# Moving attention's square sum, weight pieces and adds in a one-core hybrid encoder layer

## The chip, the cores and the metric

The kernel runs on one core of one Trainium2 chip. The metric is device time in microseconds (us) of one execution; the figure given is the median of several runs.

## The reference

One layer over 1024 rows of width 1024: a combined input projection, a spatial gating unit and a sliding-window attention side by side, each normalised and sent through one output projection, then a SwiGLU feed-forward part and a final norm.

```python
h = rms_norm(x, mix_norm_g[l])
proj = h @ w_in[l]
u_a, v_a, q, k, v = jnp.split(proj, splits, axis=-1)
y_a = spatial_gating(u_a, v_a, sgu_ln_g[l], sgu_ln_b[l], sgu_w[l], sgu_b[l])
y_b = window_sink_attention(q, k, v, sinks[l], rel_bias)
y_a = rms_norm(y_a, group_norm_g[l, :D_A])
y_b = rms_norm(y_b, group_norm_g[l, D_A:])
x = x + jnp.concatenate([y_a, y_b], axis=-1) @ w_out[l]
h = rms_norm(x, ffn_norm_g[l])
x = x + (jax.nn.silu(h @ w_gate[l]) * (h @ w_up[l])) @ w_down[l]
...
return rms_norm(x, final_norm_g)
```

## The kernel before, in words

Every fp32 product is made of three matmuls on parts rounded to fp32r: high by high, high by low, low by high (`split_mm`, L853 to L855). ScalarE makes a high part by a copy, VectorE the low part by a subtraction. So each operand is a raw tile, a ScalarE operation and a VectorE operation, and TensorE waits on a counting semaphore for the last of them.

The work of each of the five engines (TensorE, VectorE, ScalarE, POOL, and SyncE, which issues nearly all DMAs) is written out by hand, one list each, and each engine goes through its list in order. Nothing is scheduled by a program. The wide matrix products (input projection of u and q, feed-forward, down projection) use a Strassen scheme with seven products P1 to P7, taken in the order P1, P2, P6, P5, P7, P3, P4. In the input part each product has four pieces i (0 and 1 are columns of q, 2 and 3 of u). P4 takes them in the order 2, 3, 0, 1.

Stages in time: gated values v and keys (to 75 us), input products with the spatial mixing (to 163 us), attention rows r = 0 to 7 interleaved with the output projection (to 285 us), the feed-forward products, the down projection.

The names that matter here, by engine.

- **TensorE.** After P4's last piece come the transposes of row 0's probabilities (`probs_T`, L1033), the logits of row 1 (L1021), the values of row 0 (L1044), and `ya_totals(0)`, which transposes the sum of squares of the gated rows. Then the output projection: `out_unit(r, n)` is 12 matmuls, n = 0, 1 on the gated half with `woA`, n = 2, 3 on the attention half with `woB`. After three of these come `probs_T(1, 0)`, `logits(2)`, `probs_T(1, 1)` and `yb_rows(0)` (L1051), which transposes POOL's sum of attention squares, and then `ya_totals(1)`.
- **VectorE.** `d_to_lo` (L1843) makes low parts of the Strassen row sums D, `product_add` (L1859) adds products in PSUM onto earlier ones, `corner` (L1875, L1877) scales a finished block, `in_weight_lo` (L1837) makes low parts of weights, `add_bias`, `maxima` and `normal_probs` (L1973, L1984, L1998) are attention's softmax, `woA_piece` and `woB_piece` (L1780, L2010) the low parts of the four pieces of each half of the output weight. Each `woA_piece` and `woB_piece` raises `wo_split` by one. `ya_lo_rows` (L1883) makes the gated rows' low part.
- **ScalarE.** `probabilities` (exponentials, L1451), `probs_to_sbuf` (L1463), `yb_to_sbuf` (L1469), `ya_square`, `ya_hi_rows`, and the high part `woB_piece` (L1496), which waits until both halves of its `woB_raw` tile have landed.
- **POOL.** `gate(g)` (L707) multiplies the gated unit, `ya_sum(n)` (L714) sums its squares, `yb_sums(r)` (L770, L774) sums the squares of attention row r in two steps, `rootA`, `root` make the inverse roots.
- **SyncE.** Its list around here: load `woA` pieces 2 and 3, then `xr[0]` and `xr[1]`, rows of x for the residual, which lie on the same memory as the raw `woA` tiles and wait for them, then `xr[2]`, then the eight half loads of `woB_raw`:

```python
for i in range(2):
    sp.wait_ge(wo_split, 3 + i)
    sp.dma_start(xr[i][:], xt[i]).then_inc(x_in[i], 16)
sp.wait_ge(prod_done, in_at("P3", 3))
sp.dma_start(xr[2][:], xt[2]).then_inc(x_in[2], 16)
for t in IN_ORDER["P4"]:
    sp.wait_ge(prod_done, in_at("P4", t))
    for g in range(KV):
        ...
        sp.dma_start(woB_raw[t][g * DH:(g + 1) * DH, :], w_out[row:row + DH, :]).then_inc(block_in[t], 16)
```

Of the kernel before, what the change touches and what calls it, by code (L numbers as in the profile page):

```python
# [24 lines left out]
def hybrid_trunk_layer(nc, x, xT, mix_gT, w_in, sgu_ln_g, sgu_ln_b, sgu_w, sgu_b, sinks, rel_bias,  # L25
# [201 lines left out]
    YA_TOTAL_AT = ((2, 4), (1, 6))  # L227
# [73 lines left out]
    with ExitStack() as ctx:  # L301
        ps = ctx.enter_context(nc.psum_tensor("ps", [P, 8, C], F32))

        def sem(name):
# [11 lines left out]
        x_sq, x_mse, x_rstd, rstd_T, roots_ready, hT_hi_ready, hT_ready = (  # L316
            sem(n) for n in ("x_sq", "x_mse", "x_rstd", "rstd_T", "roots_ready", "hT_hi_ready", "hT_ready"))
# [45 lines left out]
        def _(sp):  # L363
# [5 lines left out]
            def xT_load(h, k):  # L369
                if h:  # L370
                    sp.wait_ge(hT_hi_ready, k + 1)
                sp.dma_start(hT_raw[h][:, k, :], xT[h, k]).then_inc(block_in[k], 16)
# [266 lines left out]
        def _(pool):  # L639
# [69 lines left out]
            def ya_sum(n):  # L709
# [4 lines left out]
                combine(V[:, dst], V[:, dst], V[:, src], ALU.add).then_inc(ya_summed, 1)  # L714
# [25 lines left out]
            ya_sum(4)  # L740
            ya_sum(5)
# [35 lines left out]
            rootA(1)  # L777
            for r in range(T):
# [9 lines left out]
                if r + 2 < T:  # L788
                    yb_sums(r + 1)
            for n, m in SUMS[0][2:5]:  # L790
# [58 lines left out]
        def _(pe):  # L849
# [29 lines left out]
            for k in range(2):  # L879
                pe.wait_ge(hT_hi_ready, k + 1)  # L880
# [91 lines left out]
            def ya_totals(half):  # L972
                slot, summed = YA_TOTAL_AT[half]
# [5 lines left out]
                for t in range(HT):  # L979
                    last = nc.tensor.transpose(ps[:, 7, t * P:(t + 1) * P], V[:, slot, t * P:(t + 1) * P], ident[:])  # L980
# [145 lines left out]
            ya_totals(1)  # L1126
            for r in range(T):
# [7 lines left out]
                if r + 1 < T:  # L1135
# [5 lines left out]
                    values(r + 1)  # L1141
                    if 0 < r < T - 2:
# [90 lines left out]
        def _(act_e):  # L1233
# [6 lines left out]
            def xT_block(h, k):  # L1240
                act_e.wait_ge(block_in[k], LOADED[k] + 16 * h)
                if h == 0 and k == 0:
                    act_e.wait_ge(wv0_in, 32)
# [22 lines left out]
            for k in range(K):  # L1266
                wv_block(k)
                xT_block(0, k)
# [171 lines left out]
            ya_square(3)  # L1440
            ya_hi_rows(3)
            in_weight_hi("P4", 2)
# [110 lines left out]
            ya_hi_rows(4)  # L1553
            ya_square(5)
            ya_hi_rows(5)
            u_gelu(7)
            probs_to_sbuf(0, 0)
# [189 lines left out]
        def _(dve):  # L1747
# [3 lines left out]
            def xT_lo(h, k):  # L1751
                dve.wait_ge(hT_hi_ready, K * h + k + 1)
# [49 lines left out]

            for k in range(K):
# [149 lines left out]
            for k in range(1, 4):  # L1953
                d_to_lo("D4", k)
            woA_piece(2)
            product_add("P3", 0)
            corner("P3", 0)
            in_weight_lo("P4", 0)
# [3 lines left out]
            woA_piece(3)  # L1962
            product_add("P3", 2)

# [43 lines left out]
            def woB_piece(t):  # L2008
                dve.wait_ge(wo_hi_ready, HA + t + 1)
                stt(woB_lo[:, t, :], woB_raw[t][:], grp_g[:, HA + t:HA + t + 1], woB_hi[:, t, :].bitcast(F32), ALU.mult, ALU.subtract).then_inc(wo_split, 1)  # L2010
# [301 lines left out]
```

## Time and profile before

| | |
|---|---|
| median of 3 runs | 927.34 us (927.29 to 927.34) |
| the profiled execution's own time | 927.43 us |
| its span in the trace | 925.6 us |
| TensorE busy | 913.2 us, 99% |
| VectorE busy | 588.2 us, 64% |
| ScalarE busy | 430.5 us, 47% |
| POOL busy | 402.2 us, 43% |
| TensorE's mean granted clock | 0.998 of full speed |

Busy time is time in which an engine executes; matmuls overlap each other in the trace, so that a matmul of 0.39 us follows the one before after 0.23 us. The span runs from the first to the last instruction in the trace; the execution's own time has some 1.8 us more around it.

### The profile page before, as it was taken

The numbers are of one execution on the slowest core, as the hardware profiler recorded it, in microseconds if no ns is written. First come the engines' busy times: TensorE is split into PE (matmuls) and PEld (weight loads), VectorE is DVE, ScalarE is ACT, GpSimd is POOL, SyncE is SP. The second block draws the span as 40 slices with busy tenths as digits, with TensorE's granted clock in tenths as the row PEclk, the third lists the DMA queues.
The fourth block names the chain that finished last, engine by engine and source line by source line (L and its number), as shares of the span: only waits on it lengthen the run. The fifth ranks groups of instructions, "written<-read, shape, count | busy, mean of one in ns | idle before, by whom it ended". The sixth has DMA issues, their size and how long they took to land.

```text
span 925.6 us, 11960 instructions
## 1 busy us (share of the span) xinstructions
PE 913.2 (99%) x4229; PEld 748.9 (81%) x4229; DVE 588.2 (64%) x776; ACT 430.5 (47%) x837; POOL 402.2 (43%) x392
## 2 busy tenths in 40 slices
PE   9999999899999999999999999999999999999997
PEld 7888887677878878888888888888888888888885
DVE  5659878877677876364464745646446666544753
ACT  6647547775655633332333333333334354444351
POOL 2459633622224388566585564955754000000022
PEclk9999999999999999999999999999999999999999
DMA  9787454112233352725527355273457996656543
GB/s 332 252 242 229 115 162 145 35 57 80 89 108 101 114 170 92 243 88 194 174 98 240 99 174 183 91 239 121 152 190 265 350 385 197 199 189 199 187 139 133
DMA packets 151487, 158.56 MB, mean 171 GB/s; under 512 B 27576, under 2 KB 109060, under 8 KB 151428
## 3 DMA queue, kind: packets, MB, share of 16 engines
q1 hardware_dynamic: 150756, 157.40, 52.5%
q8 instruction: 34, 0.56, 0.2%
q10 hardware_dynamic: 672, 0.40, 0.1%
q14 instruction: 25, 0.20, 0.1%
HBM read 117.26 MB, written 40.50 MB: 170 GB/s over the span
## 4 chain that ended last, share of the span: by engine, by line
PE 87%; DVE 4%; issue 3%; ACT 3%; POOL 2%; DMA 1%; DVEq 0%; POOLq 0%; ACTq 0%
PE ps L853 27%; PE ps L855 27%; PE ps L854 27%; ACT S L1451 1%; PE ps L969 1%; PE ps L1044 1%; PE ps L1116 1%; PE ps L1021 1%; PE ps L1033 1%; DVE P_lo L2086 1%; DMA A22s<-in_w_gate 1%; DVE woA_lo L1780 0%; POOL V L714 0%; PE ps L877 0%; DVE T_lo L2073 0%
## 5 line engine op out<-in xcount | busy, mean ns | idle before, releaser
L2086 DVE TENSOR_TENSOR P_lo<-P_raw,P_hi 128x512 fp32r<-128x512 f32 x132 | 120.8, 931 | 83.5 <-ACT P_hi L1545 76.2
L853 PE MATMUL ps<-T_hi,P_hi 128*128 128x512 f32 x352 | 137.1, 390 | 0.0
L855 PE MATMUL ps<-T_hi,P_lo 128*128 128x512 f32 x352 | 137.0, 389 | 0.0
L854 PE MATMUL ps<-T_lo,P_hi 128*128 128x512 f32 x352 | 136.9, 389 | 0.0
L797 POOL TENSOR_TENSOR wd<-wd 128x256 f32<-128x256 f32 x88 | 81.2, 923 | 93.8 <-DMA wd<-in_w_down 88.6
L853 PE MATMUL ps<-rb_hi,ra_hi 128*128 128x512 f32 x308 | 119.8, 389 | 0.0
L854 PE MATMUL ps<-rb_lo,ra_hi 128*128 128x512 f32 x308 | 119.8, 389 | 0.0
L855 PE MATMUL ps<-rb_hi,ra_lo 128*128 128x512 f32 x308 | 119.8, 389 | 0.0
L1659 ACT ACTIVATE ra_hi<-ra 128x512 fp32r<-128x512 f32 x77 | 48.6, 632 | 98.4 <-DMA rb<-w_down_T 59.6
L647 POOL TENSOR_SCALAR late<-late 128x1 f32<-128x1 f32 x12 | 5.5, 458 | 193.4 <-ACT junk L1727 177.2
L2182 DVE TENSOR_TENSOR ra_lo<-ra,ra_hi 128x512 fp32r<-128x512 f32 x77 | 55.2, 718 | 37.2 <-ACT ra_hi L1659 37.0
L1545 ACT ACTIVATE P_hi<-P_raw 128x512 fp32r<-128x512 f32 x132 | 76.6, 620 | 3.5 <-POOL P_raw L756 3.5
L853 PEld LDWEIGHTS ps<-T_hi,P_hi 128*128 128x128 f32 x352 | 66.1, 188 | 14.3 <-issue 0.7
L855 PEld LDWEIGHTS ps<-T_hi,P_lo 128*128 128x128 f32 x352 | 66.1, 188 | 13.9
L854 PEld LDWEIGHTS ps<-T_lo,P_hi 128*128 128x128 f32 x352 | 66.1, 188 | 13.6
L1650 ACT ACTIVATE G<-G 128x512 f32<-128x512 f32 x33 | 20.9, 632 | 112.4 <-DVE G L2162 112.4
L853 PE MATMUL ps<-B,P_hi 128*128 128x512 f32 x176 | 69.0, 392 | 0.1
L855 PE MATMUL ps<-B,P_lo 128*128 128x512 f32 x176 | 68.5, 389 | 0.0
L854 PE MATMUL ps<-B,P_hi 128*128 128x512 f32 x176 | 68.5, 389 | 0.0
L854 PEld LDWEIGHTS ps<-rb_lo,ra_hi 128*128 128x128 f32 x308 | 57.8, 188 | 12.1
L853 PEld LDWEIGHTS ps<-rb_hi,ra_hi 128*128 128x128 f32 x308 | 57.8, 188 | 12.1
L855 PEld LDWEIGHTS ps<-rb_hi,ra_lo 128*128 128x128 f32 x308 | 57.8, 188 | 11.8
(272 smaller groups left out, 2028.0 us busy)
## 6 DMA issues: line engine op xcount, KB each, us to landing
wd<-in_w_down SPq DMA_DIRECT2D x44, 256.0 KB, 3.4
w_down_T<-wd SPq DMA_DIRECT2D x22, 512.0 KB, 4.8
ra<-act_S SPq DMA_DIRECT2D x44, 256.0 KB, 2.7
rb<-w_down_T SPq DMA_DIRECT2D x44, 256.0 KB, 3.0
act_S<-Q SPq DMA_DIRECT2D x33, 256.0 KB, 3.7
ra<-act_A SPq DMA_DIRECT2D x33, 256.0 KB, 4.9
rb<-in_w_down SPq DMA_DIRECT2D x33, 256.0 KB, 5.7
P_raw<-in_w_gate SPq DMA_DIRECT2D x22, 256.0 KB, 3.6
```

Of the source, the lines that this page charges most:

```text
L797: nc.gpsimd.tensor_tensor(wd[:, d, :], wd[:, x, :], wd[:, y, :], ALU.subtract).then_inc(wd_summed, 1)
L853: mm(dst, lhs[0], rhs[0], start=start, stop=False, skip_group_check=onto)
L854: mm(dst, lhs[0], rhs[1], start=False, stop=False, skip_group_check=onto)
L855: return mm(dst, lhs[1], rhs[0], start=False, stop=stop, skip_group_check=onto)
L969: last = mm(ps[:, MIX_BANK[m % 2], t * P:(t + 1) * P], vn[:, h, HT * half + t], sgu_wT[:, h, :], start=True, stop=True)
L1021: last = mm(ps[:, 3 + g, (2 * ci + tp) * P:(2 * ci + tp + 1) * P], q, kT[rows, c * CH:c * CH + WIN], start=True, stop=True)
L1033: last = nc.tensor.transpose(ps[:, 5, (2 * g + tp) * P:(2 * g + tp + 1) * P], S[:, g, ci, tp, :], ident[:])
L1545: actv(w_h[p, m][:], src[:], ACT.Copy).then_inc(w_hi_ready, 1)
L1650: actv(g[:], g[:], ACT.Silu).then_inc(silu_done, 1)
L1659: actv(ra_hi[n][:], ra[n][:], ACT.Copy).then_inc(step_hi, 1)
L2086: tt(w_l[p, m][:], src[:], w_h[p, m][:].bitcast(F32), ALU.subtract).then_inc(w_split, 1)
L2182: tt(ra_lo[n][:], ra[n][:], ra_hi[n][:].bitcast(F32), ALU.subtract)
```

## The change

It has seven parts.

1. At the start VectorE, not ScalarE, makes the first block of `hT_hi`, with a semaphore of its own (`hT0_hi_ready`); the counts of `hT_hi_ready` fall by one where they are waited for.
2. VectorE: `product_add("P3", 0)` and its corner move ahead of D4's pieces 2 and 3, `in_weight_lo("P4", 2)` ahead of `add_bias(0)`.
3. VectorE: `woA_piece(2)` and `woA_piece(3)` move from among P3's adds to behind `normal_probs(0)`.
4. ScalarE: `in_weight_hi("P4", 2)` moves ahead of `ya_hi_rows(3)`, `probs_to_sbuf(0, 0)` ahead of `ya_square(5)`.
5. POOL: `yb_sums(0)` moves ahead of `ya_sum(4)` and `ya_sum(5)`, the latter writes to `roots[1]` now, and `rootA(1)` moves into the loop of rows.
6. TensorE: `ya_totals(1)` moves behind `values(1)`, and VectorE's `ya_total_sums(1)` behind `yb_lo(1)`.
7. VectorE's `woB_piece(2)` waits for all gated sums, since its low part lies on their memory.

VectorE before, from the second D4 piece of P3's time to the end of `maxima(0)`; `woA_lo` is `woA_piece`, `U` P3's sum, `s_lo` P4's weight parts, `S` the logits:

```order
L1843 TENSOR_TENSOR D_lo<-D_raw,D_hi 128x512 [waits combo_hi] x3
L1780 SCALAR_TENSOR_TENSOR woA_lo<-raw_75,small,woA_hi 128x1024 [waits wo_hi_ready]
L1859 TENSOR_TENSOR U<-ps,U 128x512 [waits c_summed,copied,prod_done]
...
L1780 SCALAR_TENSOR_TENSOR woA_lo<-raw_76,small,woA_hi 128x1024 [waits wo_hi_ready]
L1859 TENSOR_TENSOR U<-ps,U 128x512 [waits c_summed,copied,prod_done]
L1973 TENSOR_TENSOR S<-ps,bias 128x512 [waits logits_done,sinks_ready,bias_in]
L1973 TENSOR_TENSOR S<-ps,bias 128x512
L1979 MEMSET S 128x2x64 [waits s_added]
L1979 MEMSET S 128x2x64
L1837 TENSOR_TENSOR s_lo_150<-s_2_114,wB_hi_138 128x512 [waits w_hi_ready,s_added]
```

VectorE with the change, from the end of the normalisation of row 0 (L2011) to the bias of row 1 (L1986):

```order
L2008 RECIPROCAL small<-small 128x8 [waits den_ready]
L2011 TENSOR_TENSOR S<-S,small 128x1024 [waits rden_ready]
L1790 SCALAR_TENSOR_TENSOR woA_lo<-raw_75,small,woA_hi 128x1024 [waits wo_hi_ready]
L1790 SCALAR_TENSOR_TENSOR woA_lo<-raw_76,small,woA_hi 128x1024 [waits wo_hi_ready]
L1896 TENSOR_TENSOR ya<-vn,ya 128x4x128 [waits ya_hi_ready]
L1888 SCALAR_TENSOR_TENSOR qT_153<-ps,roots_81 128x8x64 [waits prod_done]
L1896 TENSOR_TENSOR ya<-vn,ya 128x4x128 [waits ya_hi_ready]
L1888 SCALAR_TENSOR_TENSOR qT_153<-ps,roots_81 128x8x64 [waits prod_done]
L1986 TENSOR_TENSOR S<-ps,bias 128x512 [waits logits_done,p_T]
```

Both `woA` pieces have left the first place and stand in the second, behind the normalisation.

SyncE's queue, the same before and with the change (172 to 174 are `xr[0]` to `xr[2]`, 168 to 171 `woB_raw[0]` to `[3]`):

```order
L464 DMA xr_172<-in_x 128x1024 [waits wo_split]
L464 DMA xr_173<-in_x 128x1024 [waits wo_split]
L466 DMA xr_174<-in_x 128x1024 [waits prod_done]
L471 DMA woB_raw_170<-in_w_out 64x1024 [waits prod_done]
L471 DMA woB_raw_170<-in_w_out 64x1024
L471 DMA woB_raw_171<-in_w_out 64x1024 [waits prod_done]
L471 DMA woB_raw_171<-in_w_out 64x1024
L471 DMA woB_raw_168<-in_w_out 64x1024 [waits prod_done]
L471 DMA woB_raw_168<-in_w_out 64x1024
```

Nothing moved in it; the first two rows wait for the two `woA` pieces.

POOL before, from the inverse root of the first half to the sum of the first attention row:

```order
L649 TENSOR_TENSOR small<-small 128x4 [waits msA_ready]
L714 TENSOR_TENSOR V<-V 128x512 [waits ya_summed,ya_squared] x2
L770 TENSOR_TENSOR yb_sq<-yb_sq 128x256 [waits yb_squared]
L774 TENSOR_TENSOR yb_sum_162<-yb_sq 128x128 [waits yb_halved]
L647 TENSOR_SCALAR small<-small 128x4 [waits ssqA_ready]
```

and with the change:

```order
L649 TENSOR_TENSOR small<-small 128x4 [waits msA_ready]
L771 TENSOR_TENSOR yb_sq<-yb_sq 128x256 [waits yb_squared]
L775 TENSOR_TENSOR yb_sum_162<-yb_sq 128x128 [waits yb_halved]
L716 TENSOR_TENSOR V<-V 128x512 [waits ya_summed,ya_squared]
L716 TENSOR_TENSOR roots_81<-V 128x512 [waits c_out,ya_summed,ya_squared]
L647 TENSOR_SCALAR small<-small 128x1 [waits yb_totalled]
```

The two gated sums now come behind the attention squares.

The diff (the declaration of the new semaphore left out):

```diff
--- before.py
+++ after.py
@@ -224,7 +224,7 @@
     SQUARE_TO = (1, 0, 2, 3, 0, 3, 0, 3)
     YA_SUMS = ((1, 0, 2), (2, 3, 4), (2, 0, 5), (2, 3, 6), (1, 0, 7), (1, 3, 8))
     YA_ROWS = (2, 3, 4, 5, 0, 1, 6, 7)
-    YA_TOTAL_AT = ((2, 4), (1, 6))
+    YA_TOTALS = ((V[:, 2], 4), (roots[1], 6))
 
     IN_PRODUCTS, W_SPLITS, W_SUMS, D_SPLIT, IN_COPIES, IN_ADDS = 32, 30, 16, 16, 12, 16
 
@@ -368,7 +368,7 @@
 
             def xT_load(h, k):
                 if h:
-                    sp.wait_ge(hT_hi_ready, k + 1)
+                    sp.wait_ge(hT_hi_ready, max(k, 1))
                 sp.dma_start(hT_raw[h][:, k, :], xT[h, k]).then_inc(block_in[k], 16)
 
             def item_load(n):
@@ -711,7 +711,9 @@
                 pool.wait_ge(ya_squared, squared)
                 if n:
                     pool.wait_ge(ya_summed, n)
-                combine(V[:, dst], V[:, dst], V[:, src], ALU.add).then_inc(ya_summed, 1)
+                if n == 5:
+                    pool.wait_ge(c_out, corner_at("P4", 1))
+                combine(roots[1][:] if n == 5 else V[:, dst], V[:, dst], V[:, src], ALU.add).then_inc(ya_summed, 1)
 
             def rootA(half):
                 cs = slice(HT * half, HT * half + HT)
@@ -737,8 +739,7 @@
             gate(6)
             gate(7)
             rootA(0)
-            ya_sum(4)
-            ya_sum(5)
+
             def w_sum(i, n, m):
                 sub = nc.gpsimd.tensor_tensor
                 if n == "S1":
@@ -774,7 +775,8 @@
                 nc.gpsimd.tensor_tensor(yb_sum4[:], yb_sq[:, 0], yb_sq[:, 1], ALU.add).then_inc(yb_summed, 1)
 
             yb_sums(0)
-            rootA(1)
+            ya_sum(4)
+            ya_sum(5)
             for r in range(T):
                 if r == T - 1:
                     pool.wait_ge(out_done, out_at(T - 1, 1))
@@ -787,6 +789,8 @@
                 root(ssqB[:, r:r + 1], msB[:, r:r + 1], rB[:, r:r + 1], DA, msB_ready, rB_ready, r + 1)
                 if r + 2 < T:
                     yb_sums(r + 1)
+                if r == 0:
+                    rootA(1)
             for n, m in SUMS[0][2:5]:
                 w_sum(0, n, m)
 
@@ -877,7 +881,10 @@
                 nc.tensor.transpose(ps[:, 0, 0:P], ident[:], ident[:])
 
             for k in range(2):
-                pe.wait_ge(hT_hi_ready, k + 1)
+                if k:
+                    pe.wait_ge(hT_hi_ready, k)
+                else:
+                    pe.wait_ge(hT0_hi_ready, 1)
                 pe.wait_ge(wv_hi_ready, k + 1)
                 for t in range(HT):
                     mm(ps[:, t, :], hT_hi[0][:, k, t * P:(t + 1) * P], wv_hi[:, k], start=k == 0, stop=False)
@@ -970,14 +977,14 @@
                 last.then_inc(mix_done, 1)
 
             def ya_totals(half):
-                slot, summed = YA_TOTAL_AT[half]
+                total, summed = YA_TOTALS[half]
                 pe.wait_ge(ya_summed, summed)
                 if half == 0:
                     pe.wait_ge(c_out, corner_at("P4", 3))
                 else:
                     pe.wait_ge(ssqA_ready, 1)
                 for t in range(HT):
-                    last = nc.tensor.transpose(ps[:, 7, t * P:(t + 1) * P], V[:, slot, t * P:(t + 1) * P], ident[:])
+                    last = nc.tensor.transpose(ps[:, 7, t * P:(t + 1) * P], total[:, t * P:(t + 1) * P], ident[:])
                 last.then_inc(ya_total, 1)
 
             def value_windows(w):
@@ -1123,7 +1130,6 @@
             logits(2)
             probs_T(1, 1)
             yb_rows(0)
-            ya_totals(1)
             for r in range(T):
                 if 0 < r < T - 1:
                     probs_T(r + 1, 0)
@@ -1139,6 +1145,8 @@
                     if r == T - 2:
                         h2_transposed(r - 1, 0)
                     values(r + 1)
+                    if r == 0:
+                        ya_totals(1)
                     if 0 < r < T - 2:
                         h2_transposed(r - 1, 1)
                 out_unit(r, 2)
@@ -1239,8 +1247,6 @@
 
             def xT_block(h, k):
                 act_e.wait_ge(block_in[k], LOADED[k] + 16 * h)
-                if h == 0 and k == 0:
-                    act_e.wait_ge(wv0_in, 32)
                 actv(hT_hi[h][:, k, :], hT_raw[h][:, k, :], ACT.Copy, scale=mix_g[:, k:k + 1]).then_inc(hT_hi_ready, 1)
 
             def wv_block(k):
@@ -1265,7 +1271,8 @@
             act_e.dma_start(mix_g, mix_gT).then_inc(wv0_in, 16)
             for k in range(K):
                 wv_block(k)
-                xT_block(0, k)
+                if k:
+                    xT_block(0, k)
             for r in range(HT):
                 xT_block(1, 2 * r)
                 square(r)
@@ -1438,8 +1445,8 @@
             ya_square(2)
             ya_hi_rows(2)
             ya_square(3)
+            in_weight_hi("P4", 2)
             ya_hi_rows(3)
-            in_weight_hi("P4", 2)
             in_weight_hi("P4", 3)
 
             def probabilities(r):
@@ -1551,10 +1558,10 @@
             u_gelu(6)
             ya_square(4)
             ya_hi_rows(4)
+            probs_to_sbuf(0, 0)
             ya_square(5)
             ya_hi_rows(5)
             u_gelu(7)
-            probs_to_sbuf(0, 0)
             probs_to_sbuf(0, 1)
             woB_piece(0)
             yb_to_sbuf(0)
@@ -1749,7 +1756,10 @@
             copy = nc.vector.tensor_copy
 
             def xT_lo(h, k):
-                dve.wait_ge(hT_hi_ready, K * h + k + 1)
+                if h or k:
+                    dve.wait_ge(hT_hi_ready, K * h + k)
+                else:
+                    dve.wait_ge(hT0_hi_ready, 1)
                 stt(hT_lo[h][:, k, :], hT_raw[h][:, k, :], mix_g[:, k:k + 1], hT_hi[h][:, k, :].bitcast(F32), ALU.mult, ALU.subtract).then_inc(hT_ready, 1)
 
             def wv_block(k):
@@ -1800,6 +1810,9 @@
                                   sinks_rep[rows].rearrange("p (g a b) -> p g a b", g=KV, a=2)[:, :, :, t2], -1.0, None, ALU.mult)
                 last.then_inc(sinks_ready, 1)
 
+            dve.wait_ge(wv0_in, 32)
+            dve.wait_ge(block_in[0], LOADED[0])
+            ts(hT_hi[0][:, 0, :], hT_raw[0][:, 0, :], mix_g[:, 0:1], None, ALU.mult).then_inc(hT0_hi_ready, 1)
             for k in range(K):
                 wv_block(k)
                 xT_lo(0, k)
@@ -1950,17 +1963,17 @@
             woA_piece(1)
             product_add("P7", 3)
             corner("P7", 3)
-            for k in range(1, 4):
-                d_to_lo("D4", k)
-            woA_piece(2)
+            d_to_lo("D4", 1)
             product_add("P3", 0)
             corner("P3", 0)
+            d_to_lo("D4", 2)
+            d_to_lo("D4", 3)
             in_weight_lo("P4", 0)
             product_add("P3", 1)
             corner("P3", 1)
             in_weight_lo("P4", 1)
-            woA_piece(3)
             product_add("P3", 2)
+            in_weight_lo("P4", 2)
 
             def add_bias(r):
                 if r == 0:
@@ -2007,6 +2020,8 @@
 
             def woB_piece(t):
                 dve.wait_ge(wo_hi_ready, HA + t + 1)
+                if t == 2:
+                    dve.wait_ge(ya_summed, 6)
                 stt(woB_lo[:, t, :], woB_raw[t][:], grp_g[:, HA + t:HA + t + 1], woB_hi[:, t, :].bitcast(F32), ALU.mult, ALU.subtract).then_inc(wo_split, 1)
 
             def add_out(r, n):
@@ -2086,7 +2101,6 @@
                 tt(w_l[p, m][:], src[:], w_h[p, m][:].bitcast(F32), ALU.subtract).then_inc(w_split, 1)
 
             add_bias(0)
-            in_weight_lo("P4", 2)
             maxima(0)
             in_weight_lo("P4", 3)
             corner("P3", 2)
@@ -2097,6 +2111,8 @@
             ya_lo_rows(3)
             corner("P4", 3)
             normal_probs(0)
+            woA_piece(2)
+            woA_piece(3)
             ya_lo_rows(4)
             corner("P4", 0)
             ya_lo_rows(5)
@@ -2118,8 +2134,6 @@
                     add_out(r + 1, 0)
                 if r + 1 < T:
                     yb_totals(r)
-                if r == 0:
-                    ya_total_sums(1)
                 if r + 2 < T:
                     add_bias(r + 2)
                     maxima(r + 2)
@@ -2131,6 +2145,8 @@
                         h2_lo(r - 1, 0)
                     add_out(r + 1, 1)
                     yb_lo(r + 1)
+                if r == 0:
+                    ya_total_sums(1)
                 add_out(r, 2)
                 if r + 2 < T:
                     normal_probs(r + 2)
```

## Rows read from the trace of the kernel before

**Rows 1.** The page's first part: busy us, share of the span, instructions.
```profile
PE 913.2 (99%) x4229; PEld 748.9 (81%) x4229; DVE 588.2 (64%) x776; ACT 430.5 (47%) x837; POOL 402.2 (43%) x392
```
**Rows 2.** Waits of TensorE: waiter, releaser, us in total, times, longest.
```profile
PE ps L1051 <- POOL yb_sum L774: 2.0, 1, 2.0
...
PE ps L1033 <- ACT pT L1463: 1.1, 1, 1.1
PE ps L853 <- DVE U L1859: 0.5, 1, 0.5
PE ps L853 <- DVE s_lo L1837: 0.3, 1, 0.3
```
**Rows 3.** Timeline of the start (start us, us, what); VectorE's TENSOR_SCALAR; xT's first landing.
```profile
4.23 0.71 ACT L1244 ACTIVATE hT_hi<-hT_raw,small 128x512 fp32r<-128x512 f32 x1
...
4.99 0.80 PE L883 MATMUL ps<-wv_hi,hT_hi 128*128 128x512 f32 x1
L1769 DVE TENSOR_SCALAR vn<-v_sb,small x8: 516/548/1559, 34.1 to 56.8; 128x512 f32<-128x512 f32 x8
DMA to landing us min/median/max: 3.0/3.0/3.0
```
**Rows 4.** Timeline of SyncE's queue, DMA issues at the start and 143 to 165 us.
```profile
1.17 0.42 SPq L372 DMA_DIRECT2D hT_raw<-in_xT  x1
...
143.24 5.38 SPq L464 DMA_DIRECT2D xr<-in_x  x2
...
154.29 9.75 SPq L471 DMA_DIRECT2D woB_raw<-in_w_out  x8
```
**Rows 5.** The loads of woB_raw: ns min/median/max of one issue, and landing.
```profile
L471 SPq DMA_DIRECT2D woB_raw<-in_w_out x8: 466/552/597, 154.3 to 163.4; - x8
DMA to landing us min/median/max: 3.4/3.8/4.2
```
**Rows 6.** Windows: full queue; one xr load; one pair of woB_raw. Last: DMA share, GB/s.
```profile
18.00:20.00 2.00, 2.00 (x11) 1.65 (x10) 0.75 (x1) 1.44 (x4) 1.25 (x5) 1.00 1.06 407
144.00:147.00 3.00, 3.00 (x14) 2.25 (x16) 2.96 (x6) 3.00 (x6) 0.00 (x0) 1.00 0.55 175
155.00:158.00 3.00, 3.00 (x15) 2.48 (x14) 2.97 (x7) 2.97 (x10) 0.00 (x0) 1.00 0.70 175
```
**Rows 7.** Timeline of VectorE, 146 to 164 us, in order of time.
```profile
146.99 1.28 DVE L1780 SCALAR_TENSOR_TENSOR woA_lo<-raw,small,woA_hi 128x1024 fp32r<-128x1024 f32 x1
...
156.38 0.69 DVE L1883 TENSOR_TENSOR ya<-vn,ya 128x512 fp32r<-128x512 f32 x1
158.06 1.23 DVE L1998 TENSOR_TENSOR S<-S,small 128x1024 f32<-128x1024 f32 x1
161.65 1.84 DVE L1883 TENSOR_TENSOR ya<-vn,ya 128x512 fp32r<-128x512 f32 x1 [2.37 <-ACT ya L1356]
```
**Rows 8.** Timeline of POOL, 147 to 178 us.
```profile
147.33 2.09 POOL L714 TENSOR_TENSOR V<-V 128x512 f32<-128x512 f32 x1 [5.87 <-ACT V L1364]
158.34 3.35 POOL L707 TENSOR_TENSOR vn<-vn,U 128x512 f32<-128x512 f32 x2 [8.91 <-ACT U L1343]
161.65 2.98 POOL L714 TENSOR_TENSOR V<-V 128x512 f32<-128x512 f32 x2
...
173.79 3.60 POOL L714 TENSOR_TENSOR V<-V 128x512 f32<-128x512 f32 x2 [2.63 <-ACT V L1364]
```
**Rows 9.** Timeline of ScalarE, 165 to 177 us.
```profile
165.18 1.14 ACT L1496 ACTIVATE woB_hi<-woB_raw,small 128x1024 fp32r<-128x1024 f32 x1
166.80 0.60 ACT L1469 ACTIVATE yb_raw<-ps 128x512 f32<-128x512 f32 x1 [0.48 <-PE ps L1044]
...
176.22 0.57 ACT L1463 ACTIVATE pT<-ps 128x512 f32<-128x512 f32 x1
```
**Rows 10.** Timeline of TensorE, 175 to 180 us.
```profile
175.39 0.60 PE L1033 MATMUL ps<-ident,S 128*128 128x128 f32 x4
...
179.65 0.33 PE L1051 MATMUL ps<-ident,yb_sum 128*128 128x128 f32 x1 [1.98 <-POOL yb_sum L774]
```

More of the change, by code:

```diff
@@ L315, in hybrid_trunk_layer @@
         x_in = [sem(f"x_in{s}") for s in range(4)]
-        x_sq, x_mse, x_rstd, rstd_T, roots_ready, hT_hi_ready, hT_ready = (
-            sem(n) for n in ("x_sq", "x_mse", "x_rstd", "rstd_T", "roots_ready", "hT_hi_ready", "hT_ready"))
+        x_sq, x_mse, x_rstd, rstd_T, roots_ready, hT0_hi_ready, hT_hi_ready, hT_ready = (
+            sem(n) for n in ("x_sq", "x_mse", "x_rstd", "rstd_T", "roots_ready", "hT0_hi_ready", "hT_hi_ready", "hT_ready"))
         block_in = [sem(f"block_in{k}") for k in range(K)]
```

## The prediction

> **What bounds the kernel now.** I read the page's first part, the waits of TensorE, and then the timelines of the stretch that they point to. TensorE is busy 913.2 of 925.6 us [rows 1], so an edit can only give back time in which TensorE stands, or add some. It stands little: 2.0 us for POOL's sum of the attention squares (L774), 1.1 us for ScalarE's copy of the probabilities (L1463), 0.5 and 0.3 us for two VectorE operations [rows 2]. All four lie between 143 and 180 us, where attention, the last input products and the first output products overlap. After 200 us no TensorE wait is listed at all, so whatever is lost or won before 180 us stays to the end. The change aims at these four and at the start.
>
> **The start.** Today ScalarE makes both operands of the first matmul in turn, the second, `hT_hi`, at 4.23 us for 0.71, and TensorE begins at 4.99 [rows 3]. Now VectorE makes `hT_hi[0]` with one TENSOR_SCALAR, whose usual length is 548 ns. It can't start before its block lands, and the earliest xT block takes 3.0 us from its issue at 1.17 [rows 3, 4], so 4.2 us. It ends at 4.75 and TensorE starts at about 4.8: **-0.2 us**. The bounds are 0 (the block lands late; VectorE then also does the two low parts later) and -0.5 (a landing at 3.7).
>
> **The four waits, if nothing else moved.** VectorE adds P3's row 0 before two of the D4 pieces and `woA_piece(2)` (-0.5). P4's third low part is made before attention's bias (-0.3), ScalarE copies the probabilities before the fifth square (-1.1), and POOL does the attention squares' sum before the two gated sums that take 3.60 us from 173.79 [rows 8] (-2.0). That is 3.9 us at most. The totals of the second half are transposed later with the same four matmuls: nothing gained or lost. The new wait of VectorE's `woB_piece(2)` for the sixth gated sum costs nothing: the gated sums come straight behind the attention squares and end 3.6 us later, and VectorE has the bias and the maxima of row 2 to do first. POOL's new wait on `c_out` is for a corner that stands ahead of row 1's bias in VectorE's list, and is long done.
>
> **What is behind the moved weight pieces.** `woA_piece(2)` and `(3)` go from the middle of P3 to behind the first row's normalisation. They are 1.28 us each [rows 7], but they also raise `wo_split` to 3 and 4, and SyncE's queue waits for exactly these before it loads `xr[0]` and `xr[1]`, since these lie on the raw weights. SyncE works in order. Today it issues the two `xr` loads from 143.24 on, the second at the end of 5.38 us, and then the eight `woB_raw` loads from 154.29 to 164.04, each as P4's products finish [rows 4]. Now all eight stand behind the fourth `woA` piece. ScalarE's next operation after the probabilities' copy is `woB_piece(0)`, on the sixth of them; today it runs at 165.18 without a wait [rows 9].
>
> When is the fourth piece done? The normalisation (L1998) starts at 158.06 and ends at 159.29 [rows 7]. Ahead of it VectorE loses a 1.28 us piece, but P4's third low part must now wait for ScalarE and for POOL's sum at 147.33 to 149.42 [rows 8], so I put its end only 0.3 earlier, at 159.0. Without interference the pieces are done at 159.0 + 2 x 1.2 = 161.4. But POOL is in its gates then (158.34, x2 in 3.35) and in sums from 161.65 [rows 8], and VectorE operations that read two SBUF tensors don't run beside POOL's: `ya_lo`, started at 161.65 together with POOL's sum, took 1.84 us, where the same operation at 156.38, with POOL idle, took 0.69 [rows 7, 8]. With one POOL operation of 1.15 us slipped in ahead of each piece it is **163.7**. I take this, since POOL has six operations queued there. The Trainium skill (GPSIMD Engine Reference, "8. Key points") says that GpSimd shares its SBUF interfaces with VectorE and contends with VectorE instructions of two SBUF inputs. By that rule both pieces are caught, the later of the two times.
>
> When does `woB_raw[0]` land? Behind the fourth piece stand `xr[1]`, `xr[2]` (0.33 us an issue) and three pairs of `woB` loads (0.55 each) [rows 4, 5]; the second half of piece 0 is issued 0.7 + 5 x 0.55 = 3.45 us later and lands 3.8 after that [rows 5]: 163.7 + 7.2 = 170.9 by issue alone. By bytes: `xr[1]`'s data begin 1.5 us after its issue, at 165.2, and five half-megabytes go before piece 0 is complete. By DMA time used they cost 3.0 x 0.55 = 1.65 us for an `xr` and 3.0 x 0.70 = 2.1 for a `woB` pair [rows 6], 9.6 in all: 174.8. At the 407 GB/s of a full queue [rows 6] 2.62 MB take 6.4: 171.6. Between 171.6 and 174.8 I take **172.8**. With the undisturbed 161.4 the same three are 168.6, 169.3 and 172.5. The Trainium skill (DMA: Bandwidth & Descriptors, "Anatomy of one DMA") gives about 2 us and bytes at 436 GB/s; for one `xr` load that is 3.2 us, as the row has it. By its rate the five take 6.0 us, the landing is 171.2 and the sum below would be 930.4, an estimate from that page.
>
> From there the order of ScalarE is fixed. `woB_piece(0)` at 165.18 to the copy of row 1's probabilities at 176.22 is 11.04 us, less 0.48 that it waited for TensorE, plus the copy's 0.57 [rows 9]; TensorE's transposes follow 0.15 later and the yb transposes 0.4 behind them. So TensorE gets to L1051 at landing + 11.7 = 184.5, where it now gets there at 179.65 [rows 10]: +4.85. It stops on the way first at row 1's probabilities (now 175.39, without a wait), since these hang on the same ScalarE work. What was won in the four waits is swallowed: TensorE is early and then stands longer. POOL's squares' sum is then hidden in it.
>
> **Sum:** 927.43 (the profiled execution) + 4.85 - 0.2 = 932.1; the median of the three runs is 0.1 lower, so **932.0**.
>
> **Rivals.**
> *Faster, the four waits go (8%).* If piece 0 lands before 167.9 (landing + 11.7 before 179.65), the loads decide nothing or little. With a landing at 165 or sooner the price is 927.3 - 3.9 - 0.2 = 923.2. For it speaks that VectorE has an idle 2.37 us before 161.65 [rows 7] into which both pieces fit, and that the queue is otherwise empty. Against it: even with these pieces undisturbed the issue times alone give 168.6. Only if VectorE came through its stretch more than 0.7 us sooner than I put it could this happen.
> *No change (14%).* VectorE keeps the port, the fourth piece ends at 161.4, and the loads are bound by issue, or go at 407 GB/s: landing 168.6 to 169.3, +0.65 to +1.35, less 0.2: 927.8 to 928.5.
> *Slower, but by VectorE and POOL themselves.* POOL's gates 4 and 5 could get in ahead of the normalisation, since ScalarE's GELU comes earlier too: then all of the above moves 1.2 us on, to 933.2, and with the slow DMA price to 935.2. This is inside my forecast (78% in all); it is its upper end.
>
> **Range and chances.** 0.2% is 1.85 us, about what a measurement tells from no change. The forecast covers 928.9 to 935.2 (landings of 170 to 176); half of the "no change" case is taken in by going down to 928.4. Slower by over 0.2% 0.78, within it 0.14, faster 0.08.
>
> **What the profile after would show.** SyncE's `xr[1]` issue at about 163.7, some 15 us later than now, and the `woB_raw` loads bunched from 164 to 168; ScalarE standing 6 to 10 us before L1503 (the `woB_hi` piece) for a DMA; TensorE standing some 5 to 7 us before the transposes of row 1's probabilities, and the yb_sum wait gone; nothing changed after 200 us but the shift. I am wrong if ScalarE's `woB_piece(0)` still starts before 168, and the size is wrong if the landing is off my 172.8, about one for one.

## Result and the profile after

The changed kernel takes 936.1 us (median of 5 runs, 935.66 to 936.47), the kernel before 927.34 (927.29 to 928.36): ratio 1.009 [1.008, 1.010] (the brackets are a 95% interval), 8.8 us slower. The forecast was 932.0, between 928.4 and 935.2: the direction held, the size was short by 4.1, and the measured time lies 0.9 above the upper end. The profiled execution of the changed kernel took 935.74 us, 8.31 more than the one of before; all that follows is made against that 8.31.

The page's first part, and the granted clock in 40 slices, of the changed kernel:

```profile
PE 914.3 (98%) x4229; PEld 750.5 (80%) x4229; DVE 588.5 (63%) x777; ACT 430.1 (46%) x836; POOL 402.3 (43%) x392
...
PEclk9999999899999999999999999999999999999999
```

The busy times are those of [rows 1] within 1.6 us; the span has grown, so the shares of TensorE, VectorE and ScalarE are each a point lower. The eighth slice of the clock, 163 to 187 us at 23.3 us a slice, has fallen to 8. Waits of TensorE after (waiter, releaser, us in total, times, longest):

```profile
PE ps L1040 <- DVE S L2011: 9.7, 2, 8.6
PE ps L881 <- POOL ident L643: 1.5, 1, 1.5
PE ps L857 <- DVE ya L1896: 1.4, 1, 1.4
```

The four waits of [rows 2] are gone; one of 8.6 us, for row 1's normalisation (L2011), has come, and two small ones: 1.1 us for row 0's normalisation and 1.4 for the gated rows' low part. (The 1.5 us for `ident` is at the very start and is in every run.) What lies behind the long one is read backwards. ScalarE (start us, us, what, idle before):

```profile
162.48 0.60 ACT L1470 ACTIVATE pT<-ps 128x512 f32<-128x512 f32 x1 [1.03 <-PE ps L1040]
174.75 1.15 ACT L1503 ACTIVATE woB_hi<-woB_raw,small 128x1024 fp32r<-128x1024 f32 x1 [11.66 <-DMA woB_raw<-in_w_out]
```

It stands 11.66 us for a load, where it had none to wait for at 165.18 [rows 9]. SyncE's queue, and the loads' time from issue to landing:

```profile
160.80 2.56 SPq L464 DMA_DIRECT2D xr<-in_x  x2
163.40 0.43 SPq L466 DMA_DIRECT2D xr<-in_x  x1
163.88 4.98 SPq L471 DMA_DIRECT2D woB_raw<-in_w_out  x8
DMA to landing us min/median/max: 5.3/7.0/8.6
```

The eight half loads, issued over 9.75 us as P4's products ended [rows 4], now go within 4.98, and land after 5.3 to 8.6 us instead of 3.4 to 4.2 [rows 5]. VectorE and POOL at the two weight pieces:

```profile
156.29 2.25 DVE L2011 TENSOR_TENSOR S<-S,small 128x1024 f32<-128x1024 f32 x1
158.47 4.54 DVE L1790 SCALAR_TENSOR_TENSOR woA_lo<-raw,small,woA_hi 128x1024 fp32r<-128x1024 f32 x2
```

```profile
156.17 3.52 POOL L707 TENSOR_TENSOR vn<-vn,U 128x512 f32<-128x512 f32 x2 [8.96 <-ACT U L1350]
159.66 4.48 POOL L716 TENSOR_TENSOR V<-V 128x512 f32<-128x512 f32 x2
```

The pieces take 4.54 us and POOL's sums 4.48 beside them, which both had in less (1.28 a piece [rows 7], 2.98 for the two sums [rows 8]). TensorE in the end:

```profile
183.46 1.11 PE L1040 MATMUL ps<-ident,S 128*128 128x128 f32 x4 [8.55 <-DVE S L2011]
184.51 2.08 PE L1028 MATMUL ps<-kT,qT 64*128 64x128 f32 x16
...
187.43 0.42 PE L1058 MATMUL ps<-ident,yb_sum 128*128 128x128 f32 x1
```

It gets to the yb transposes at 187.43 where it got there at 179.65 [rows 10]: +7.78. The same four transposes of `S` take 1.11 us, not 0.60 [rows 10], and the windows (from and to in us, length, busy us and instructions of TensorE, its weight loads, VectorE, ScalarE and POOL) say why (last three columns: granted clock, DMA share, GB/s):

```profile
174.00:179.00 5.00, 0.91 (x5) 0.41 (x3) 1.93 (x3) 4.19 (x7) 0.00 (x0) 1.00 0.34 77
179.00:183.00 4.00, 0.00 (x0) 0.00 (x0) 1.81 (x4) 4.00 (x18) 0.77 (x1) 0.55 0.00 0
183.00:189.00 6.00, 5.54 (x29) 4.69 (x30) 4.97 (x7) 4.39 (x6) 5.43 (x6) 0.50 0.01 3
189.00:192.00 3.00, 3.00 (x16) 2.16 (x16) 2.90 (x5) 1.14 (x6) 0.10 (x1) 0.90 0.00 0
```

While TensorE stood, its granted clock fell to the lower level, 0.50 of 2.4 GHz, and stayed there for the first 6 us from 183.

### The profile page after: what moved, and what is told of

Read it like the earlier page. It is cut to its first block, busy times and chain, and to the rows that moved or that the text cites. A ratio compares the mean times of both kernels' runs of the same rounds, so it can differ in the third digit from the quotient of the medians.

```text
span 933.9 us, 11960 instructions
## 1 busy us (share of the span) xinstructions
PE 914.3 (98%) x4229; PEld 750.5 (80%) x4229; DVE 588.5 (63%) x777; ACT 430.1 (46%) x836; POOL 402.3 (43%) x392
## 4 chain that ended last, share of the span: by engine, by line
PE 90%; DVE 4%; issue 2%; ACT 1%; DMA 1%; POOL 1%; SPq 0%; DVEq 0%; POOLq 0%; ACTq 0%
PE ps L857 28%; PE ps L859 28%; PE ps L858 28%; PE ps L1123 1%; DMA woB_raw<-in_w_out 1%; PE ps L1040 1%; PE ps L976 1%; PE ps L1051 1%; PE ps L1028 1%; DVE S L2011 1%; DMA A22s<-in_w_gate 1%; DVE woA_lo L1790 0%; DVE P_lo L2101 0%; PE ps L881 0%; DVE T_lo L2088 0%
```

## Experiments

The kernel before had medians of 927.73, 927.61, 927.59 and 927.10 us in the sessions of these runs; each ratio is to the runs of its own session. The changed kernel's 936.1 was measured beside a 927.34, so the differences to it that follow cross sessions whose medians of the same kernel lie up to 0.4 us apart.

**1. The weight pieces.** Before with only those moved, then the changed kernel with only those put back.

```diff
# e1, on the kernel before
-            woA_piece(2)
             product_add("P3", 0)
...
-            woA_piece(3)
...
             normal_probs(0)
+            woA_piece(2)
+            woA_piece(3)
# e2, on the changed kernel
             normal_probs(0)
-            woA_piece(2)
-            woA_piece(3)
...
             d_to_lo("D4", 3)
+            woA_piece(2)
...
             in_weight_lo("P4", 1)
+            woA_piece(3)
```

> The kernel before with only the two woA pieces of VectorE moved behind the first normalisation. Theory (the queue of SyncE): the loads of woB_raw are held until the fourth piece is done, piece 0 lands near 174 us, ScalarE stands some 9 us before its woB piece and TensorE some 7 to 8 us before the transposes of row 1's probabilities; about 935 to 936 us, as slow as the whole change or slower by little. Rival (VectorE and POOL hold each other up, or the moved POOL sums do it): at most 929 us, with woB_raw landing in time.

> The whole change with the two woA pieces put back among P3's adds. Theory: the loads go out as before, the wait for row 1's probabilities disappears, and what is left are the gains of the other parts: start -1.4, P3's sum and P4's weight -0.8, the probabilities' copy -1.1, POOL's sum -2.0: about 922 us. Rival (another part costs too): above 925 us.

The move alone: 935.51 us, ratio 1.0077 [1.0061, 1.0094]. The pieces put back: 923.82 us, ratio 0.9955 [0.9940, 0.9970]. So the two pieces cost 7.8 us by themselves and 12.3 in the company of the rest, and the rest is worth 3.9 (927.73 to 923.82), which TensorE's long stand swallows. In e1 TensorE waits

```profile
PE ps L1033 <- DVE S L1996: 6.2, 1, 6.2
PE ps L1033 <- ACT pT L1463: 2.1, 1, 2.1
```

and ScalarE's first `woB_hi` starts at 173.48, 11.75 us behind the end of the fourth piece (157.18 + 4.55); in the changed kernel the distance is 11.74.

**2. SyncE's queue.** The changed kernel with the loads of `xr[0]` and `xr[1]` behind the weights' in SyncE's list, so that nothing but P4 holds those up, while the pieces stay where the change put them.

```diff
-            for i in range(2):
-                sp.wait_ge(wo_split, 3 + i)
-                sp.dma_start(xr[i][:], xt[i]).then_inc(x_in[i], 16)
             sp.wait_ge(prod_done, in_at("P3", 3))
...
+            for i in range(2):
+                sp.wait_ge(wo_split, 3 + i)
+                sp.dma_start(xr[i][:], xt[i]).then_inc(x_in[i], 16)
```

> The whole change, with the two xr loads of SyncE put behind the eight woB_raw loads, so that those don't wait for the woA pieces. Theory: woB_raw lands as before, ScalarE doesn't stand, and the time is 924 to 925 us, since TensorE still waits 1.2 us for the normalisation and 1.4 us for ya_lo, which the moved pieces push behind POOL's operations. Rival (the place of the pieces on VectorE is the cost): still above 930 us.

926.86 us, ratio 0.9990 [0.9981, 0.9999]: of the 12.3 us the queue's order gives back 9.2. I had expected 2 to 3 us more. The load's wait is gone (ScalarE starts `woB_hi` at 164.01 without one), but waits for VectorE have stayed:

```profile
PE ps L1040 <- DVE S L2011: 2.8, 2, 1.6
PE ps L857 <- DVE ya L1896: 1.4, 1, 1.4
```

The pieces still hold VectorE for 4.54 us (at 159.50), so that row 1's bias starts at 167.93, where in e2 it starts at 164.52, and its normalisation comes late. Of the 2.8 us, 1.2 are for row 0's normalisation and are in e2 as well; the other 1.6 and the 1.4 for `ya` are the pieces' own price. They match the 3.0 us between e3 and e2. It stood nowhere in my working; in the changed kernel the long stand swallows them.

**3. The clock.** The changed kernel with 76 more transposes of the identity into a bank that is rewritten next, ahead of row 1's transposes, so that TensorE doesn't stand. They add work and change nothing that is computed.

```diff
             out_unit(1, 0)
+            for n in range(76):
+                nc.tensor.transpose(ps[:, 5, 0:P], ident[:], ident[:])
             probs_T(1, 0)
```

> The whole change, with 76 transposes of the identity into a free bank ahead of the transposes of row 1's probabilities, so that TensorE works through most of its 8.6 us wait. Theory: the matmuls after the wait keep their full pace, and some 2 us come back: about 934 us. Rival (the slower pace behind the wait costs nothing that counts): 936 us.

934.12 us, ratio 1.0068 [1.0053, 1.0083], 2.0 less than the changed kernel, though row 1's transposes start no sooner (183.61, against 183.46). From there to the second values it takes 5.87 us, against 7.93. The windows that fell to 0.50 above:

```profile
179.00:183.00 4.00, 4.00 (x39) 4.00 (x37) 1.80 (x4) 4.00 (x18) 0.62 (x1) 1.00 0.00 0
183.00:189.00 6.00, 5.19 (x41) 4.19 (x40) 5.97 (x8) 4.43 (x6) 5.62 (x6) 1.00 0.00 0
```

So the lower clock behind the stand cost 2.0 us on top of the stand itself.

**4. The rate of the weights' loads.** In the changed kernel the `woB_raw` half loads run at 221 to 258 GB/s (168 to 175 us) with all 16 DMA engines busy, where the row of x before them ran at 406. Two edits ask whether the shape is the cause: one transfer of 128 partitions for each weight tile, and two of 64 for each of the first two rows of x.

```diff
# e9, on the changed kernel
-                for g in range(KV):
-                    row = DA + (g * G + t) * DH
-                    sp.dma_start(woB_raw[t][g * DH:(g + 1) * DH, :], w_out[row:row + DH, :]).then_inc(block_in[t], 16)
+                sp.dma_start(woB_raw[t][:], woB_src[:, t]).then_inc(block_in[t], 16)
# ScalarE's count for a tile falls from 32 to 16, and
# woB_src = w_out[DA:DA + KV * G * DH, :].rearrange("(g t d) n -> g t d n", g=KV, t=G)
# e11, on the changed kernel
-                sp.dma_start(xr[i][:], xt[i]).then_inc(x_in[i], 16)
+                for q in range(2):
+                    hp = slice(64 * q, 64 * q + 64)
+                    sp.dma_start(xr[i][hp, :], xt[i][hp, :]).then_inc(x_in[i], 16)
# VectorE's counts for these rows rise by 16
```

> The changed kernel with each tile of the raw weights of the attention half loaded by one transfer of 128 partitions in place of two of 64. Theory (the half transfers drain at 240 GB/s although all 16 DMA engines are busy, since each has only 64 partitions of 4 KB): whole transfers drain nearer the 406 GB/s of the x loads, a tile takes about 1.5 us in place of 2.15, the tile that ScalarE waits for is the third and lands 1.3 to 2 us sooner, and the time is 934.1 to 934.8. Rival (the rate has to do with where the data lie in memory, not with the shape): 936.1 as the changed kernel, and the same 240 GB/s.

> The changed kernel with the first two rows of x for the residual loaded by two transfers of 64 partitions each in place of one of 128; the weights' loads as in the changed kernel. Theory (the shape of 64 partitions sets the 240 GB/s of the weights' half loads, not their source): the second x row, issued at 163, now drains at some 240 GB/s where 406 were seen at 165 to 166, so the weights behind it land about 0.9 us later and the time is about 937. Rival (the rate belongs to the source tensor): the x rows still drain at 400, the landing stays within 0.3 us and the time is 936.1 to 936.4.

The first went wrong in a way that no theory had: 961.86 us, ratio 1.0370 [1.0356, 1.0385]. ScalarE waits until 197.97, and the windows show why:

```profile
170.00:180.00 10.00, 4.89 (x22) 3.73 (x20) 0.35 (x1) 0.00 (x0) 1.22 (x2) 0.94 0.13 52
180.00:190.00 10.00, 0.00 (x0) 0.00 (x0) 0.00 (x0) 0.00 (x0) 0.00 (x0) 0.50 0.13 53
```

A DMA share of 0.13 is two engines of 16. The source of the new transfer has two blocks of 64 rows, so its outermost count is 2. The Trainium skill (DMA: Bandwidth & Descriptors, "Why a DMA increments its semaphore by 16 and not by 1") says that a transfer runs on the largest number of engines, up to 16, that divides the outermost counts of both sides; here that is 2, and the trace agrees. As a test of the rate the run is void.

The second answers it. Bandwidth of the changed kernel at 165 us, one row of x in whole transfers, and of e11 at 165 to 167, the same row in halves:

```profile
165.00:166.00 1.00, 0.14 (x2) 0.00 (x0) 1.00 (x2) 0.00 (x0) 1.00 (x2) 1.00 1.00 406
```

```profile
165.00:166.00 1.00, 0.80 (x6) 0.42 (x4) 1.00 (x3) 0.00 (x0) 1.00 (x1) 1.00 0.86 242
166.00:167.00 1.00, 0.00 (x0) 0.00 (x0) 1.00 (x2) 0.00 (x0) 1.00 (x2) 1.00 1.14 254
```

937.54 us, ratio 1.0112 [1.0096, 1.0127]: 1.4 more than the changed kernel, where 0.9 was expected. The weights land 13.2 us behind the fourth piece in place of 11.7. A half is also a smaller transfer, 256 KB. That isn't the cause: from 5 to 10 us the changed kernel loads tiles of 128x512, 256 KB each over 128 partitions, at 356 GB/s:

```profile
5.00:10.00 5.00, 5.00 (x22) 4.08 (x23) 3.67 (x6) 3.00 (x5) 0.00 (x0) 1.00 1.00 356
```

So the 64-partition shape sets the rate, whatever the source. The Trainium skill (SBUF — State Buffer, "Door 1: The DMA port swizzle") says that partitions 0 to 63, and likewise 64 to 127, reach only 8 of the 16 ports of the memory, some 218 GB/s. The rows show 221 to 258, with halves of both kinds in the queue: somewhat above that figure, and far below 406.

**5. What each wait is worth.** Before with POOL's part alone (its lists, the moved totals), with ScalarE's copy alone, with the start alone, and with two more of the warm-up transposes ahead of the first matmul.

```diff
# e7, on the kernel before (with the moves of the totals and the wait of woB_piece(2))
-            ya_sum(4)
-            ya_sum(5)
...
             yb_sums(0)
-            rootA(1)
+            ya_sum(4)
+            ya_sum(5)
# e8, on the kernel before
+            probs_to_sbuf(0, 0)
             ya_square(5)
             ya_hi_rows(5)
             u_gelu(7)
-            probs_to_sbuf(0, 0)
# e4, on the kernel before: the change's part 1 as it is
# e5, on the kernel before
-    WARM = 15
+    WARM = 17
```

> The kernel before with POOL's part of the change alone: the first attention row's sum of squares ahead of the last two sums of gated squares, and the totals of the second half behind the second values. Theory (each wait of TensorE is worth its own length while nothing else stands in the way): the wait of 2.0 us for that sum goes, nothing takes its place, so 925.6 beside the 927.6 of the kernel before. Rival (TensorE runs at the next wait sooner and gives it back, or the moved totals stand in the way of the second row): 927.0 to 927.6. The 3.8 us that the change won with the weight pieces put back would then have to come from somewhere else.

> The kernel before with ScalarE's copy of the first row's probabilities ahead of the sixth square of the gated rows, and nothing else. Theory: TensorE's wait of 1.1 us for the copy goes and the time is 926.5. Rival: the sum of the attention squares hangs on POOL, which is tied up until 177.4 whatever TensorE does, so TensorE stands 1.1 us longer there and the time stays 927.6; the two waits then are one.

> The kernel before with only the start changed (VectorE makes the first block of hT_hi). After this change the whole program stood 1.4 us earlier at 140 us, where 0.2 was predicted. Theory: the start alone gives 1.4 us, 926.0 us, because the first matmuls run at full pace. Rival: it gives 0.2 us, and the rest came from elsewhere.

> The kernel before with 17 instead of 15 warm-up transposes, which fill the 0.4 us in which TensorE stood before its first real matmul. If that gap is what makes the first matmuls slow, this alone gives about 1.1 us (926.2 us), with the operand no earlier than before. If not, nothing or a small loss (927.3 to 927.5 us).

| edit | median us | ratio, interval |
|---|---|---|
| e7, POOL's part | 924.46 | 0.9967 [0.9954, 0.9979] |
| e8, the copy | 927.59 | 0.9999 [0.9990, 1.0008] |
| e4, the start | 927.64 | 0.9997 [0.9988, 1.0006] |
| e5, warm-up | 927.22 | 0.9999 [0.9989, 1.0009] |

POOL's part alone brings 3.1 of the 3.9 us (by the interval, 1.9 to 4.3), and the wait was 2.0. From row 1's probability transposes to the second values TensorE took 7.69 us (175.39 to 183.08) and takes 5.08 (174.24 to 179.32): 2.0 is the wait, and some 0.5 the totals' transposes, which aren't saved but come behind the values now (0.4 us, from 180.33). So about 1 us of the 3.1 is left over. It may be the clock: of the 16 executions of the kernel before that were timed beside e7 and e8, the seven with a mean granted clock of 0.998, as the profiled one has, have a median of 926.9 us, and the nine with 0.996 or 0.997 one of 927.75. In e4 and e8 the lower clock is seen to follow such a wait (below). No trace of those nine executions is kept, so this isn't shown.

The copy's wait of 1.1 us is worth nothing alone. The rival was right that TensorE would run into POOL's queue, but not where: it stands for VectorE's normalisation, which POOL held up, and no longer for POOL's sum. Waits of TensorE in e8, and its VectorE and POOL:

```profile
PE ps L1033 <- DVE S L1998: 2.6, 1, 2.6
```

```profile
172.53 1.27 DVE L1993 TENSOR_TENSOR small<-small 128x8 f32<-128x8 f32 x1
173.84 0.20 DVE L1995 RECIPROCAL small<-small 128x8 f32<-128x8 f32 x1
174.07 2.20 DVE L1998 TENSOR_TENSOR S<-S,small 128x1024 f32<-128x1024 f32 x1
```

```profile
172.42 2.77 POOL L714 TENSOR_TENSOR V<-V 128x512 f32<-128x512 f32 x2 [1.89 <-ACT V L1364]
```

POOL's sums of gated squares come 1.4 us sooner than in [rows 8] and now meet the normalisation, which takes 2.20 us in place of 1.23 [rows 7]. An operation on 8 numbers a partition, 0.16 us in the kernel before, takes 1.27 there too.

The waits are still 0.5 us shorter in sum (2.6 against 1.1 + 2.0). That and more went to the clock: it fell to 0.50 at 178 to 180 us, and from row 1's transposes to the second values TensorE took 7.17 us (176.33 to 183.50), against 7.69 less the 1.98 of waiting, 5.71, in the kernel before. The one execution of e8 whose mean clock was 0.999 took 926.06 us; the ten others, at 0.996 or 0.997, took 927.02 to 927.87. So e8's zero is one shorter wait and one fallen clock, not proof that the copy's wait was worth nothing.

**6. A better version.** e2 with POOL's fifth gate waiting for the normalisation that it held up, and then the first `woB_lo` ahead of VectorE's first addition.

```diff
# e10, on e2
             ya_sum(1)
+            pool.wait_ge(pn_ready, 1)
             gate(4)
# e12, on e10
-            add_out(0, 0)
             woB_piece(0)
+            add_out(0, 0)
             normal_probs(1)
```

> The changed kernel with the weight pieces put back (923.8) and POOL's fifth gate made to wait for the first row's normalisation. Theory (VectorE's normalisation took 2.25 us in place of 1.23 because POOL's gate started 0.1 us before it and the two cannot run side by side): it takes 1.2 again, TensorE's wait of 1.2 us for it goes to about 0.2, and the time is 922.8. Rival (POOL's later gates hold up the squares and the gated rows, and so the first output products): the wait only moves, 923.8 or a little more.

> The kernel with the weight pieces put back and the gate made to wait (924.4), and on VectorE the low part of the first attention weight ahead of the first addition of output products. Theory (TensorE's last wait of 1.3 us, for the second row's normalisation, comes from VectorE's queue: the addition stands 1.3 us for a root from POOL while the low part, ready since 164.9, stands behind it; put first it fills that gap): the normalisation starts 1.0 to 1.3 us sooner, at about 171.6 in place of 172.8, TensorE's wait for it falls to 0.3 or less, and the time is 923.1 to 923.3. Rival (ScalarE's exponentials, done at 170.5, or POOL's sum at 171.2 hold the normalisation up instead): 924.4.

e10: 924.36 us, ratio 0.9969 [0.9956, 0.9981]; e12: 923.97 us, ratio 0.9964 [0.9951, 0.9976]. Neither can be told from e2. In e10 the first half of the theory came true and the gain did not, as the rival had it:

```profile
156.65 1.23 DVE L2014 TENSOR_TENSOR S<-S,small 128x1024 f32<-128x1024 f32 x1
```

The normalisation takes 1.23 us again instead of 2.25, but TensorE's wait of 1.2 us only moves to row 1's (1.5 in all, the longest 1.3). In e12 it shrinks to 0.9; the addition still waits 1.03 us for POOL's root, which took 1.94 instead of 1.03 beside `woB_lo`: one engine's gap was filled with work that slowed the other. The version with the lowest median is e2, the change without the move of the weight pieces: 3.9 us faster than the kernel before, 12.3 faster than the changed one. The ratios of e7, e10 and e12 lie within its interval.

## Why the prediction was right in sign and short in size

- **The mechanism held, link by link.** The pieces behind the normalisation, SyncE's queue behind the pieces, ScalarE behind the loads, row 1 behind ScalarE: every sign named for it is there, two of them larger than I put them (ScalarE stands 11.7 us for a forecast of 6 to 10, TensorE 8.6 for 5 to 7), and e1, e2 and e3 show by edits that the pieces and SyncE's queue are the first two links. The links behind them are read from the traces. After 200 us nothing changes but the shift: row 2's transposes are 8.36 us later, and the end 8.31.
- **The fourth piece**: forecast 163.7, measured 163.01 (158.47 + 4.54). The term of one POOL operation ahead of each piece was right within 0.2: forecast 4.7 us from the normalisation, measured 4.54. By the Trainium skill's rule on two SBUF inputs beside POOL (GPSIMD Engine Reference, "8. Key points") both pieces are caught, and they were: 4.54 us for two that took 1.28 each in the kernel before.
- **The landing of `woB_raw[0]`** was the first wrong step: forecast 172.8, measured 174.75, and 2.6 us longer from the piece's end than I put it (11.74 against 9.1). I had a price from DMA time used and one at 407 GB/s, and took a value between them. The two were no bounds of one unknown: 407 belongs to transfers of 128 partitions, and the half loads drain at 240. [rows 6] had it: a pair of half loads moved 175 GB/s at a DMA share of 0.70, which is 250 for a full share. That the 9.6 us by DMA time used gives 174.8 is partly luck, since the data began 0.7 us sooner. From 162 to 174.75 the windows have some 260 KB more than the six tiles that had to be complete (three rows of x, three of weights). If the transfers are served in the order of their issue, which no row shows, about 1 us lies between the last byte and ScalarE's start, for which I had no term. The Trainium skill's 436 GB/s (DMA: Bandwidth & Descriptors, "Anatomy of one DMA"), by which I had estimated a landing at 171.2, holds for no half load here.
- **The clock** was the second wrong step: it was missing altogether, a term put at nothing. I forecast a stand of 5 to 7 us and priced the work behind it at full speed. The yb transposes came 12.7 us behind ScalarE's start on the landed weights, not 11.7; in e6, at full clock, they came 11.6 behind it, so the 11.7 was right. From there the second values took 3.96 us, where e6, at full clock, took 2.97: 2.0 us in all, the number of e6.
- **The sum, put right**: 4.85 + 1.95 for the landing + 1.0 for the clock up to the yb transposes = 7.8; then 1.0 for the clock, less 0.5 for the totals that moved out of the stretch = 8.3, at the second values, where the profile has 8.31. The totals come right behind them, and where the shift settles, at row 2's transposes, it is 8.36.
- **The start**, forecast -0.2: TensorE begins at 4.79, as forecast (4.8), and e4 can't be told from nothing (927.64 against 927.61, interval -1.1 to +0.6 us). The profile of the changed kernel is 1.1 us sooner than that of the kernel before at a landmark, the first mixing transposes. That is mostly chance: TensorE gets there at 21.4 to 22.5 us in the nine executions with the new start, mean 21.7, and at 21.7 to 22.6 in the five with the old, mean 22.2. It doesn't enter the sum, since TensorE then waits for the loads anyhow.
- **The four waits**: 3.9 us "if nothing else moved" is just what e2 gained, but not for my reasons. The waits for POOL and for the copy hung on one queue and weren't two terms: with the copy's wait gone, TensorE stood 2.6 us where it had stood 1.1 + 2.0 (e8), and POOL's part alone brings most of the gain (e7). Nor were they bare waits: the clock that can fall behind them was no term of mine.
- **The rivals.** The faster case needed a landing before 167.9; e3 makes it and gets 926.9, not 923.2, since VectorE's own lateness was not in it. POOL's gates did get in beside the normalisation (2.25 us for 1.23), which was my upper end's 1.2. The case of no change needed the two pieces undisturbed; they took 4.54 us. My lower end didn't follow from its own sum: a landing at 170 gives 929.2, not 928.9.

## What to carry to other kernels

Before moving an operation, follow every counter that it raises into the DMA queues: a load that waits for it holds all loads behind it, whatever they wait for themselves. Price a queue of transfers by rows of the same shape, not by the fullest rate in the trace, and price a stand of TensorE with the work behind it at the lower clock (here 2.0 us behind a stand of 8.6). And take waits on a chain that shares one engine as one term: removing the first can be worth nothing while the engine behind the last is no sooner.

## What the runs showed that I had not expected

- The clock can fall behind a wait of 2.0 us too, though it didn't in the profiled execution of the kernel before. In e4 TensorE waits for POOL's sum as in [rows 2], and the work behind it ran at the lower level:

```profile
178.00:179.00 1.00, 0.70 (x6) 0.71 (x7) 0.29 (x1) 0.00 (x0) 0.24 (x1) 1.00 0.00 0
179.00:180.00 1.00, 1.00 (x5) 0.76 (x4) 0.90 (x2) 0.00 (x0) 0.12 (x1) 0.60 0.00 0
180.00:181.00 1.00, 1.00 (x4) 0.81 (x3) 0.99 (x2) 0.00 (x0) 0.92 (x2) 0.50 0.00 0
```

  It had been 1.35 us ahead of the kernel before at the yb transposes (178.30 against 179.65) and was 0.25 behind at the second values (183.33 against 183.08). It fell behind the 2.6 us wait of e8 as well, and in e1 behind the 2.1 us for the copy (0.50 at 164 to 166 us) before it fell again behind the 6.2. It did not in e5, which has the 2.0 us wait too. Why it fell in some and not in others stays open.
- The first four matmuls take 2.08 us in the profile of the kernel before and 1.40 in that of the changed one, but the change isn't the cause. Two more warm-up transposes (e5) left them at 2.06; over all profiles they take 1.19 to 2.08 with the old start (1.19 in e7) and 1.20 to 2.07 with the new one (2.07 in e3 and e12). So it differs between executions; from what was not found.
- One transfer for each weight tile in place of two halves cost 26 us (e9), since it ran on two DMA engines of 16.
